# A decoder trunk on one core: the output banks of the feed-forward rotate in a fixed way, and one of the four weight sums of each quad is made by an adding DMA that GpSimd issues

## The chip, the cores and the metric

The kernel runs on one core of a Trainium2 chip. The metric is device time in microseconds (us) of one execution; the median of several runs is compared. All data are fp32.

## What is computed

A trunk of two layers on 256 tokens of width 2048. The mixers differ (retention and pooling in layer 0, windowed attention in layer 1), and the change does not touch them. What it touches is the feed-forward that follows each mixer, with 5632 hidden channels:

```python
def conv_glu_ffn(x, w_in, conv_w, conv_b, w_out):
    S = x.shape[1]
    h = x @ w_in                                    # 2048 -> 2*5632
    hp = jnp.pad(h, ((0, 0), (CONV_WIDTH - 1, 0), (0, 0)))
    hc = conv_b + hp[:, 0:S] * conv_w[0]
    for kk in range(1, CONV_WIDTH):
        hc = hc + hp[:, kk:kk + S] * conv_w[kk]
    gate, val = jnp.split(hc, 2, axis=-1)
    return (jax.nn.gelu(gate, approximate=False) * val) @ w_out
```

## The kernel before

**Precision in two parts.** TensorE multiplies in a rounded fp32 form. So each operand is split into a high part (ScalarE copies it into that form: `high`, L564, for weights) and a low part (VectorE subtracts the high part from the original: `low`, L921), and three products (high by high, low by high, high by low) make one.

**Weights** come in blocks of 1 MB (128 partitions, 4 rows of 512 columns each), numbered by a step `s`. SyncE loads them (`load`, L406) one after the other into a ring `raw` of six slots; a slot is loaded again when TensorE has used the block that was in it (semaphore `used`). ScalarE and VectorE work on blocks four and three steps ahead of TensorE (`HI_LEAD`, `LO_LEAD`). Each engine goes through its instructions in order.

**The feed-forward of a layer** is cut into 11 chunks of 512 hidden channels. A chunk c has a gate part (`G_AT[c]`, four steps) and a value part (`V_AT[c]`, four steps). In each, TensorE makes the hidden values of both in four PSUM banks (`hidden`, L1555 and L1565); ScalarE copies one half of the result out (`halves`, L628, called by `kind_halves`), VectorE adds the other (`pair_sum`, L951, called by `kind_sums`), and both do the convolution (L733 on ScalarE, L1183 on VectorE), the gelu (L706) and the product of gate and value.

**The output product** runs on two finished chunks at a time, a duo p. It takes a 2x2 scheme with seven products in place of eight: `quad(q, ...)`, one over the first half of the output columns (at `Q_AT[p]`, after the value part of chunk a = 2p+2) and one over the second (at `C_AT[p]`, after the value part of chunk b = 2p+3). There are 18 quads in all: five first and four second ones in each layer; the last duo's second half is made plainly by `pair_output`. The seven products (steps q to q+6) use W_11, W_22 and W_21 as loaded and four sums of the blocks:

```
SUM_12  = W_11 + W_12'          (arena)     first_weight_sum, L1245
SUM_24  = W_12' + W_22          (in place, in the ring slot of W_12')  weight_sums, L1251
SUM_124 = SUM_12 + W_22         (arena)     weight_sums, L1254
SUM_ALL = SUM_124 + W_21        (arena)     last_weight_sum, L1261
```

where W_12' is the block loaded at step `q + SUM_24`. All four are made by VectorE; the steps of the sums that go into the products wait on the semaphore `summed` in `high`. The activations' combinations ("forms": L1217 to L1233, L746, L1211) are made in the gate part of chunk a. Each product is read from PSUM and added to the residual `xres` by `take_product` (L1271), nine reads in a quad, counted by `quad_read`. VectorE makes the first three sums within `gate_and_sums`, while TensorE is in the value part before the quad; the three `low` of steps q, q+1 and q+2 stand behind them.

**Banks.** Eight banks, used as two sets of four, 0 to 3 and 4 to 7. Before the change a first quad of duo p has its products in set x = 4 (p % 2), and the gate part of chunk b, which follows it, goes into the same set x; so TensorE waits there until VectorE has read the quad (`quad_read`, r+7 and r+9), or, in the last duo, so does `pair_output`. The value part of chunk a stands in the other set y, and VectorE adds it (`kind_sums(a, 1, y)`) after the quad.

Of the kernel before, what the change touches and what calls it, by code (L numbers as in the profile page):

```python
# [22 lines left out]
ALU = mybir.AluOpType  # L23
# [80 lines left out]

SUM_12, W_11, SUM_24, W_22, SUM_124, W_21, SUM_ALL = range(PRODUCTS)
SUM_PLACES = {SUM_12: 1, SUM_124: 0, SUM_ALL: 1}
SUM_COUNTS = {SUM_12: 1, SUM_24: 2, SUM_124: 3, SUM_ALL: 4}
QUADS = [(l, p, n) for l in range(2) for p in range(DUOS) for n in ((0, 1) if p < DUOS - 1 else (0,))]
QUAD_AT = [S_FFN[l] + (Q_AT[p] if n == 0 else C_AT[p]) for l, p, n in QUADS]
SUMS = {s + i: (i, 4 * k + n) for k, s in enumerate(QUAD_AT) for i, n in SUM_COUNTS.items()}  # L110
SLOT_OF = [s for s in range(S_END) if s not in SUMS or SUMS[s][0] == SUM_24]
LOAD_OF = {s: i for i, s in enumerate(SLOT_OF)}

# [50 lines left out]
def build_trunk(nc, x, ln_gain, ln_bias, even_w_in, pool_w, pool_scale, even_w_out, attn_w_qkv, attn_b_qkv,  # L164
# [10 lines left out]
    with ExitStack() as ctx:  # L175
# [137 lines left out]
        g_ready = sem("g_ready")  # L313
        ffn_added = sem("ffn_added")
        summed = sem("summed")
        formed = sem("formed")
        form_hi = sem("form_hi")
        form_ready = sem("form_ready")
# [214 lines left out]
        @block.gpsimd  # L533
        def _(pool):
            nc.gpsimd.memset(ident[:], 0.0).then_inc(ident_ready, 1)
            pool.wait_ge(ident_ready, 1)
            nc.gpsimd.affine_select(out=ident[:], in_=ident[:], compare_op=ALU.not_equal, fill=1.0, base=0,
                                    pattern=[[-1, P]], channel_multiplier=1).then_inc(ident_ready, 1)


            pool.wait_ge(gain_ready, 4)
            for i, n in enumerate((2, 3)):
                c = slice(COLS * n, COLS * n + COLS)
                pool.wait_ge(last_normed, i + 1)
                pool.wait_ge(last_first, 1)
                nc.gpsimd.tensor_tensor(xres[:, 0, c], xres[:, 0, c], lnp[:, 0, c], ALU.mult).then_inc(pool_step, 1)
                pool.wait_ge(pool_step, i + 1)
                nc.gpsimd.tensor_tensor(xres[:, 0, c], xres[:, 0, c], lnp[:, 1, c], ALU.add).then_inc(last_scaled, 1)
# [3 lines left out]
        def _(act):  # L552
            def high(s):

                if s >= S_END:
                    return
                if s in SUMS:
                    act.wait_ge(summed, SUMS[s][1])
                else:
                    act.wait_ge(*landed(s))  # L560
                if s >= RING:

                    act.wait_ge(used, s - RING + 1)
                nc.scalar.activation(w_hi[:, s % RING], raw_at(s), ACT.Copy).then_inc(hi_ready, 1)  # L564
# [144 lines left out]
            def feed_forward(l):  # L709
# [76 lines left out]
                            form_high(0, f)  # L786

                for p in range(DUOS):
                    a, b, x = 2 * p + 2, 2 * p + 3, 4 * (p % 2)
                    y = 4 - x  # L790
                    s = base + G_AT[a]
                    if p == 0:
                        kind_halves(1, 1, 4, s)
                    first_taps(a - 1, 1)
                    for j in range(KG):
                        high(s + j + HI_LEAD)
                        if p > 0 and j == 0:
                            act.wait_ge(used, s)
                            for f in forms_of(p)[:-5]:
                                form_high(p, f)  # L800
                        if j == 2:
                            form_high(p, X_12)
                            form_high(p, X_22)
                        if j == 3:
                            for f in (D_1, D_2, D_4):
                                form_high(p, f)
                    s = base + V_AT[a]
                    kind_halves(a, 0, x, s)
                    first_taps(a, 0)
                    for j in range(KG):  # L810
                        high(s + j + HI_LEAD)
                        if j in (1, 2):
                            chunk_gelu(a, j - 1)
                    kind_halves(a, 1, y, base + V_AT[a] + KG)
                    s = base + Q_AT[p]
                    for j in range(PRODUCTS):
                        high(s + j + HI_LEAD)
                    first_taps(a, 1)
                    if b < FC:
                        s = base + G_AT[b]  # L820
                        for j in range(KG):
                            high(s + j + HI_LEAD)
                        s = base + V_AT[b]
                        kind_halves(b, 0, x, s)
                        first_taps(b, 0)
                        for j in range(KG):
                            high(s + j + HI_LEAD)
                            if j in (1, 2):
                                chunk_gelu(b, j - 1)
                        s = base + C_AT[p]  # L830
                        kind_halves(b, 1, y, s)
                        for j in range(PRODUCTS):
                            high(s + j + HI_LEAD)

# [71 lines left out]
        def _(dve):  # L906
# [257 lines left out]
            def feed_forward(l):  # L1164
# [83 lines left out]
                def weight_sums(q):  # L1248

                    dve.wait_ge(*landed(q + W_22))  # L1250
                    vec.tensor_tensor(raw_at(q + SUM_24), raw_at(q + SUM_24), raw_at(q + W_22), ALU.add) \  # L1251
                        .then_inc(summed, 1)
                    dve.wait_ge(summed, 4 * QUAD_AT.index(q) + 1)
                    vec.tensor_tensor(raw_at(q + SUM_124), raw_at(q + SUM_12), raw_at(q + W_22), ALU.add) \  # L1254
                        .then_inc(summed, 1)

                def last_weight_sum(q):

                    dve.wait_ge(*landed(q + W_21))
                    dve.wait_ge(summed, 4 * QUAD_AT.index(q) + 3)  # L1260
                    vec.tensor_tensor(raw_at(q + SUM_ALL), raw_at(q + SUM_124), raw_at(q + W_21), ALU.add) \  # L1261
                        .then_inc(summed, 1)

# [67 lines left out]
                        first_forms(0)  # L1331

                for p in range(DUOS):
                    a, b, x = 2 * p + 2, 2 * p + 3, 4 * (p % 2)
                    y = 4 - x
                    s = base + G_AT[a]
                    if p == 0:
                        kind_sums(1, 1, 4)
# [3 lines left out]
                    for j in range(KG):  # L1342
# [4 lines left out]
                            second_forms(p)  # L1347
                        if j == 3:
                            last_forms(p)
                    gate_and_sums(base + V_AT[a], a, x, base + Q_AT[p])  # L1350
                    quad(base + Q_AT[p], x)
                    if b < FC:
                        s = base + G_AT[b]
                        kind_sums(a, 1, y)
                        for j in range(KG):
                            low(s + j + LO_LEAD)
                            if j < 2:
                                value_pair(a, j)
                        gate_and_sums(base + V_AT[b], b, x, base + C_AT[p])
                        kind_sums(b, 1, y)  # L1360
                        quad(base + C_AT[p], x)

                tail, c = base + TAIL_AT, FC - 1
                s = base + C_AT[DUOS - 1]
                kind_sums(c, 1, 4)
                for j in range(KG):
                    if j < 2:
                        value_pair(c, j)
                    low(s + j + LO_LEAD)
                    if j == 1:  # L1370
                        gated_low(0)
                    if j == 2:
                        gated_low(1)
                        dve.wait_ge(used, s + 2)
                        add_chunk(2, 0, ffn_added)
                dve.wait_ge(used, tail)
                add_chunk(3, 2, ffn_added)
                low(tail + LO_LEAD)

                m, out0, s1 = 2 * l + 1, outs + 2, tail + NCH  # L1380
# [152 lines left out]
        def _(pe):  # L1533
# [355 lines left out]
            def feed_forward(l):  # L1889
# [60 lines left out]
                hidden(G_AT[1], 0, evicted(0, 0))  # L1950
                hidden(V_AT[1], 4, evicted(0, 1))
                for p in range(DUOS):
                    a, b, x = 2 * p + 2, 2 * p + 3, 4 * (p % 2)
                    y, q = 4 - x, base + Q_AT[p]
                    r = READS * QUAD_AT.index(q)
                    hidden(G_AT[a], x, evicted(a - 1, 0 if p == 0 else 1))
                    hidden(V_AT[a], y, evicted(1, 1) if p == 0 else ((quad_read, r - 2), (quad_read, r)))
                    quad(q, x, p, evicted(a, 0))
                    waits = ((quad_read, r + 7), (quad_read, r + READS))
                    if b < FC:  # L1960
                        hidden(G_AT[b], x, waits)
                        hidden(V_AT[b], y, evicted(a, 1))
                        quad(base + C_AT[p], x, p, evicted(b, 0))
                    else:
                        pair_output(p, x, waits)

                s, c = base + TAIL_AT, FC - 1
                pe.wait_ge(g_ready, 2 * l + 2)
                pe.wait_ge(*evicted(c, 1)[1])
                ready(s)  # L1970
                for a in range(TOK):
                    ins = plain_tile(s, T, 0, last_bank(0) + a, a, True, True)
# [148 lines left out]
```

## Time and profile before

| | us |
|---|---|
| median of 3 runs | 2020.44 (2020.44 to 2020.65) |
| the profiled execution | 2020.72 |
| its span | 2018.9 |
| busy: TensorE (PE) / VectorE (DVE) / ScalarE (ACT) / GpSimd (POOL) | 2005.5 / 1689.0 / 1081.6 / 5.8 |
| idle of TensorE in the span | 13.4 |

How to read it: "PE" is the matmuls, "PEld" the weight loads of TensorE, which overlap them; "SPq" is SyncE's DMA queue. The time of an execution is that of its span and 1.8 us around it. The rows further down give starts in us from the span's start, durations in us, and in brackets how long an engine sat idle before the row and what ended that. A matmul's row is longer than the distance to the next one's start, since matmuls are pipelined; the pace of TensorE is read from the starts.

### The profile page before, as it was taken

The page shows a single profiled execution, that of the slowest core. Times are in us where ns is not written, and L with a number is a line of the kernel's source. Part 1 is how long each engine was busy: PE and PEld are TensorE (multiplying, and loading weights), DVE is VectorE, ACT ScalarE, POOL GpSimd, SP SyncE. Part 2 cuts the span into 40 slices and gives each one's busy share as a digit, 9 for nine tenths or more (in the row PEclk, how much of TensorE's full clock was granted, in tenths as well). Part 3 has the DMA queues.
Part 4 walks back from the last instruction along what each step waited for, and adds up shares of the span by engine and source line. Part 5 has one row for each costly group of instructions (what it writes and reads, how often), then busy time and mean ns, then how long its engine had stood idle before and what let it go on. Part 6 is the DMA issues. An engine that isn't in the chain of part 4 may idle for free.

```text
span 2018.9 us, 25760 instructions
## 1 busy us (share of the span) xinstructions
PE 2005.5 (99%) x10708; PEld 1715.5 (85%) x10708; DVE 1689.0 (84%) x1705; ACT 1081.6 (54%) x1087; POOL 5.8 (0%) x10
## 2 busy tenths in 40 slices
PE   9999999999999999999999999999999999999998
PEld 8888888888888888888888877888888888888886
DVE  5446566769899998999997786776989999899998
ACT  5443444555655656556544664455565565655653
POOL 0000000000000000000000000000000000000001
PEclk9999999999999999999999999999999999999999
DMA  9654464656656556556656345465665655655662
GB/s 330 194 189 153 158 236 160 208 188 200 214 172 207 196 200 203 193 189 208 225 194 197 127 133 188 158 208 188 203 213 171 205 199 197 205 191 190 207 226 107
DMA packets 194824, 390.39 MB, mean 193 GB/s; under 512 B 6970, under 2 KB 9748, under 8 KB 193684
## 3 DMA queue, kind: packets, MB, share of 16 engines
q1 hardware_dynamic: 194419, 388.49, 57.8%
q8 instruction: 84, 1.38, 0.3%
q10 hardware_dynamic: 288, 0.26, 0.1%
q14 instruction: 33, 0.26, 0.0%
HBM read 386.36 MB, written 2.10 MB: 192 GB/s over the span
## 4 chain that ended last, share of the span: by engine, by line
PE 66%; DVE 27%; issue 5%; DMA 1%; ACT 0%; SPq 0%; DVEq 0%
PE ps L1555 26%; PE ps L1565 13%; DVE w_lo L921 9%; PE ps L1582 6%; PE ps L1584 5%; PE ps L1583 5%; DVE sum_lo L921 4%; DVE xres L1271 3%; DVE arena L1183 2%; PE ps L1884 2%; PE ps L1885 2%; PE ps L1886 2%; DVE forms L1211 1%; DVE arena L951 1%; DVE arena L1254 1%
## 5 line engine op out<-in xcount | busy, mean ns | idle before, releaser
L921 DVE TENSOR_TENSOR w_lo<-raw,w_hi 128x2048 fp32r<-128x2048 f32 x352 | 797.0, 2284 | 61.2 <-ACT w_hi L564 60.9
L564 ACT ACTIVATE w_hi<-raw 128x2048 fp32r<-128x2048 f32 x352 | 664.4, 1910 | 261.5 <-DMA raw<-ffn_w_in 100.5
L1555 PE MATMUL ps<-T,w_hi 128*128 128x512 f32 x3264 | 765.4, 390 | 2.9 <-DVE xres L1271 2.9
L1555 PEld LDWEIGHTS ps<-T,w_hi 128*128 128x128 f32 x3264 | 605.2, 188 | 128.0 <-issue 7.0
L1565 PEld LDWEIGHTS ps<-T,w_lo 128*128 128x128 f32 x3264 | 405.8, 191 | 10.0 <-issue 2.0
L1565 PE MATMUL ps<-T,w_lo 128*128 128x256 f32 x3264 | 410.6, 283 | 0.0
L1884 PE MATMUL ps<-w_hi,forms 128*128 128x512 f32 x464 | 180.5, 389 | 0.0
L1886 PE MATMUL ps<-w_hi,forms 128*128 128x512 f32 x464 | 180.5, 389 | 0.0
L1582 PE MATMUL ps<-w_hi,T 128*128 128x512 f32 (+1 forms) x448 | 177.3, 396 | 0.2
L1584 PE MATMUL ps<-w_hi,T 128*128 128x512 f32 (+1 forms) x448 | 173.8, 388 | 0.0
L1583 PE MATMUL ps<-w_lo,T 128*128 128x512 f32 (+1 forms) x448 | 173.6, 387 | 0.0
L564 ACT ACTIVATE w_hi<-arena 128x2048 fp32r<-128x2048 f32 x54 | 103.8, 1923 | 122.2 <-DVE arena L1245 83.2
L1183 DVE SCALAR_TENSOR_TENSOR arena<-arena,taps 128x256 f32<-128x256 f32 x352 | 154.6, 481 | 8.2 <-ACT arena L733 5.1
L733 ACT ACTIVATE arena<-arena,taps 128x256 f32<-128x256 f32 x176 | 91.6, 593 | 122.2 <-DVE arena L951 122.2
L951 DVE TENSOR_TENSOR arena<-ps,half 128x512 f32<-128x512 f32 x96 | 61.8, 685 | 100.2 <-ACT half L628 100.2
L628 ACT ACTIVATE half<-ps 128x512 f32<-128x512 f32 x104 | 56.3, 593 | 152.8 <-PE ps L1555 152.8
L921 DVE TENSOR_TENSOR sum_lo<-arena,w_hi 128x2048 fp32r<-128x2048 f32 x54 | 123.4, 2285 | 0.0
L1271 DVE SCALAR_TENSOR_TENSOR xres<-ps,xres 128x512 f32<-128x512 f32 x162 | 104.9, 684 | 3.0 <-PE ps L1886 3.0
L1884 PEld LDWEIGHTS ps<-w_hi,forms 128*128 128x128 f32 x464 | 87.1, 188 | 18.0
L1886 PEld LDWEIGHTS ps<-w_hi,forms 128*128 128x128 f32 x464 | 87.1, 188 | 18.0
L1582 PEld LDWEIGHTS ps<-w_hi,T 128*128 128x128 f32 x448 | 84.2, 188 | 19.8 <-DVE T L1012 2.8
L1584 PEld LDWEIGHTS ps<-w_hi,T 128*128 128x128 f32 x448 | 84.1, 188 | 17.6
(185 smaller groups left out, 1640.1 us busy)
## 6 DMA issues: line engine op xcount, KB each, us to landing
raw<-ffn_w_in SPq DMA_DIRECT2D x176, 1024.0 KB, 5.1
raw<-ffn_w_out SPq DMA_DIRECT2D x88, 1024.0 KB, 5.1
raw<-even_w_in SPq DMA_DIRECT2D x38, 1024.0 KB, 5.1
raw<-attn_w_qkv SPq DMA_DIRECT2D x20, 1024.0 KB, 5.1
raw<-even_w_out SPq DMA_DIRECT2D x16, 1024.0 KB, 5.1
raw<-attn_w_out SPq DMA_DIRECT2D x16, 1024.0 KB, 5.1
arena<-ln_gain SPq DMA_DIRECT2D x4, 1024.0 KB, 4.9
arena<-ln_bias SPq DMA_DIRECT2D x4, 1024.0 KB, 7.2
```

Of the source, the lines that this page charges most:

```text
L564: nc.scalar.activation(w_hi[:, s % RING], raw_at(s), ACT.Copy).then_inc(hi_ready, 1)
L733: ins = nc.scalar.activation(to[:, t], h[:, t, 0:SEQ], ACT.Identity, bias=taps[:, 4 * l + 3, at:at + 1], scale=taps[:, 4 * l, at:at + 1])
L921: vec.tensor_tensor(lo_at(s), raw_at(s), w_hi[:, s % RING].bitcast(F32), ALU.subtract).then_inc(lo_ready, 1)
L1183: ins = vec.scalar_tensor_tensor(conv[:, i], h[:, i, k:k + SEQ], tap(k), conv[:, i], ALU.mult, ALU.add)
L1271: vec.scalar_tensor_tensor(xres[:, a, c], ps[:, bank], sign / ALPHA, xres[:, a, c], ALU.mult, ALU.add).then_inc(quad_read, 1)
L1555: ins = mm(ps[:, banks[j]], w_hi[:, s % RING, k, P * j:P * j + P], T[:, GK * kg + k], start=kg == 0 and k == 0, stop=kg == KG - 1 and k == ...
L1565: ins = mm(ps[:, banks[j], 0:SEQ], lo_at(s)[:, k, P * j:P * j + P], T[:, GK * kg + k, 0:SEQ], start=False, stop=False)
L1582: mm(ps[:, bank, 0:n], x_hi, w_hi[:, s % RING, k, c], start=start and k == 0, stop=False)
L1583: mm(ps[:, bank, 0:n], x_hi, lo_at(s)[:, k, c], start=False, stop=False)
L1584: ins = mm(ps[:, bank, 0:n], x_lo, w_hi[:, s % RING, k, c], start=False, stop=stop and k == GK - 1)
L1884: mm(ps[:, bank], x_hi, w, start=start and k == 0, stop=False, skip_group_check=more)
L1886: ins = mm(ps[:, bank], x_lo, w, start=False, stop=last, skip_group_check=more)
```

## The change

Two things, in every feed-forward:

1. **Banks.** The sets no longer alternate with p. The gate part of a is in 0 to 3, its value part in 4 to 7, the first quad in 0 to 3, the gate part of b in 4 to 7, its value part in 0 to 3, the second quad in 4 to 7. The gate part of b now waits until the value part of a has been evicted, the value part of b waits for the reads of the first quad. `kind_sums(a, 1, 4)` and `kind_sums(b, 1, 0)` stand ahead of the quad in VectorE's order. `pair_output` and what follows it move to 4 to 7 too.
2. **SUM_24.** VectorE's addition (L1251) goes. In its place GpSimd issues two DMAs that read W_22 from HBM once more and add it to the ring slot that holds W_12' (each two of the four rows, 512 KB). The first waits until W_12' has landed and until SUM_12 has been made (which reads the same slot); the second waits until the first has landed. ScalarE's `high` of the step q+2 waits for both (`second_summed`).

```diff
-SUM_COUNTS = {SUM_12: 1, SUM_24: 2, SUM_124: 3, SUM_ALL: 4}
+SUM_COUNTS = {SUM_12: 1, SUM_24: 0, SUM_124: 2, SUM_ALL: 3}
...
 (GpSimd)
+            for k, (l, p, n) in enumerate(QUADS):
+                to = raw_at(QUAD_AT[k] + SUM_24)
+                pool.wait_ge(*landed(QUAD_AT[k] + SUM_24))
+                pool.wait_ge(summed, 3 * k + 1)
+                for j in range(2):
+                    t, c = GK * (2 * p + 1) + 2 * j, COLS * (2 * n + 1)
+                    pool.dma_start(to[:, 2 * j:2 * j + 2], w_ffn_out[l][:, t:t + 2, c:c + COLS],
+                                   accum_op=ALU.add).then_inc(second_summed, 16)
+                    pool.wait_ge(second_summed, 32 * k + 16 * (j + 1))
...
 (ScalarE, high)
-                if s in SUMS:
+                if s in SUMS and SUMS[s][0] == SUM_24:
+                    act.wait_ge(second_summed, 32 * (QUAD_AT.index(s - SUM_24) + 1))
+                elif s in SUMS:
                     act.wait_ge(summed, SUMS[s][1])
...
 (VectorE, weight_sums)
                     dve.wait_ge(*landed(q + W_22))
-                    vec.tensor_tensor(raw_at(q + SUM_24), raw_at(q + SUM_24), raw_at(q + W_22), ALU.add) \
-                        .then_inc(summed, 1)
...
 (VectorE, the loop over duos)
-                    gate_and_sums(base + V_AT[a], a, x, base + Q_AT[p])
-                    quad(base + Q_AT[p], x)
+                    gate_and_sums(base + V_AT[a], a, 0, base + Q_AT[p])
+                    kind_sums(a, 1, 4)
+                    quad(base + Q_AT[p], 0)
                     if b < FC:
                         s = base + G_AT[b]
-                        kind_sums(a, 1, y)
...
-                add_chunk(3, 2, ffn_added)
+                add_chunk(3, 6, ffn_added)
...
 (TensorE, the loop over duos)
-                    hidden(G_AT[a], x, evicted(a - 1, 0 if p == 0 else 1))
-                    hidden(V_AT[a], y, evicted(1, 1) if p == 0 else ((quad_read, r - 2), (quad_read, r)))
-                    quad(q, x, p, evicted(a, 0))
+                    hidden(G_AT[a], 0, evicted(a - 1, 0 if p == 0 else 1))
+                    hidden(V_AT[a], 4, evicted(1, 1) if p == 0 else ((quad_read, r - 2), (quad_read, r)))
+                    quad(q, 0, p, evicted(a, 0))
                     waits = ((quad_read, r + 7), (quad_read, r + READS))
                     if b < FC:
-                        hidden(G_AT[b], x, waits)
-                        hidden(V_AT[b], y, evicted(a, 1))
-                        quad(base + C_AT[p], x, p, evicted(b, 0))
+                        hidden(G_AT[b], 4, evicted(a, 1))
+                        hidden(V_AT[b], 0, waits)
+                        quad(base + C_AT[p], 4, p, evicted(b, 0))
                     else:
-                        pair_output(p, x, waits)
+                        pair_output(p, 4, evicted(a, 1))
```

The rest is the same bank numbers on ScalarE's side, the counts of `summed` (three to a quad), and in the tail a wait on `ffn_added` in place of the last eviction.

## Rows read from the trace of the kernel before

**Rows 1.** The page: busy time of each engine, and TensorE's granted clock in 40 slices.
```profile
PE 2005.5 (99%) x10708; PEld 1715.5 (85%) x10708; DVE 1689.0 (84%) x1705; ACT 1081.6 (54%) x1087; POOL 5.8 (0%) x10
...
PEclk9999999999999999999999999999999999999999
```

**Rows 2.** TensorE's waits: line, releaser, total us, times, longest us.
```profile
PE ps L1555 <- DVE xres L1271: 2.9, 6, 0.5
PE ps L1884 <- DVE xres L1271: 1.8, 2, 0.9
```

**Rows 3.** Timeline, PE: around a gate part, and around pair_output.
```profile
877.62 0.39 PE L1885 MATMUL ps<-sum_lo,forms 128*128 128x512 f32 x1
877.85 0.39 PE L1886 MATMUL ps<-w_hi,forms 128*128 128x512 f32 x1
878.72 1.63 PE L1555 MATMUL ps<-T,w_hi 128*128 128x512 f32 x6 [0.49 <-DVE xres L1271]
...
1005.61 0.39 PE L1886 MATMUL ps<-w_hi,forms 128*128 128x512 f32 x1
1006.90 0.47 PE L1884 MATMUL ps<-w_hi,gT 128*128 128x512 f32 x1 [0.90 <-DVE xres L1271]
```

**Rows 4.** Timeline, DVE, ahead of and in the second quad at 923 us.
```profile
907.02 2.28 DVE L1245 TENSOR_TENSOR arena<-raw 128x2048 f32<-128x2048 f32 x1
...
912.07 2.29 DVE L1251 TENSOR_TENSOR raw<-raw 128x2048 f32<-128x2048 f32 x1 [1.06 <-DMA raw<-ffn_w_out]
...
918.68 4.49 DVE L921 TENSOR_TENSOR w_lo<-raw,w_hi 128x2048 fp32r<-128x2048 f32 x2
924.13 1.29 DVE L951 TENSOR_TENSOR arena<-ps,half 128x512 f32<-128x512 f32 x2 [0.96 <-ACT half L628]
...
930.34 2.29 DVE L921 TENSOR_TENSOR sum_lo<-arena,w_hi 128x2048 fp32r<-128x2048 f32 x1
```

**Rows 5.** Timeline, ACT, of the same stretch.
```profile
914.39 1.92 ACT L564 ACTIVATE w_hi<-raw 128x2048 fp32r<-128x2048 f32 x1 [0.82 <-DVE raw L1251]
916.22 0.61 ACT L706 ACTIVATE arena<-arena 128x512 f32<-128x512 f32 x1
...
923.50 1.09 ACT L628 ACTIVATE half<-ps 128x512 f32<-128x512 f32 x2 [4.86 <-PE ps L1555]
```

**Rows 6.** Timeline, PE: the first matmuls of this quad and of its second step.
```profile
923.30 0.39 PE L1884 MATMUL ps<-w_hi,forms 128*128 128x512 f32 x1
...
926.02 0.39 PE L1884 MATMUL ps<-w_hi,gT 128*128 128x512 f32 x1
```

**Rows 7.** Timeline, DVE, ahead of the first quad at 987 us.
```profile
969.23 1.28 DVE L951 TENSOR_TENSOR arena<-ps,half 128x512 f32<-128x512 f32 x2
...
974.34 2.29 DVE L1245 TENSOR_TENSOR arena<-raw 128x2048 f32<-128x2048 f32 x1
...
984.86 6.69 DVE L921 TENSOR_TENSOR w_lo<-raw,w_hi 128x2048 fp32r<-128x2048 f32 x3
```

**Rows 8.** Timeline, PE: the first matmul of that quad.
```profile
986.79 0.39 PE L1884 MATMUL ps<-w_hi,forms 128*128 128x512 f32 x1
```

**Rows 9.** Timelines, DVE and PE: SUM_12 and quad start at 460 and at 591 us.
```profile
460.26 2.29 DVE L1245 TENSOR_TENSOR arena<-raw 128x2048 f32<-128x2048 f32 x1
...
476.54 0.39 PE L1884 MATMUL ps<-w_hi,forms 128*128 128x512 f32 x1
...
590.66 2.29 DVE L1245 TENSOR_TENSOR arena<-raw 128x2048 f32<-128x2048 f32 x1
...
603.53 0.39 PE L1884 MATMUL ps<-w_hi,forms 128*128 128x512 f32 x1
```

**Rows 10.** The page: a DMA queue (packets, MB, share), and issues with us to landing.
```profile
q1 hardware_dynamic: 194419, 388.49, 57.8%
...
raw<-ffn_w_out SPq DMA_DIRECT2D x88, 1024.0 KB, 5.1
```

**Rows 11.** The DMA issues: a store of half a block from SBUF.
```profile
out<-xres SPq DMA_DIRECT2D x2, 512.0 KB, 2.7
```

**Rows 12.** Busy time by stretch; the last two are DMA share and GB/s.
```profile
912.00:918.00 6.00, 6.00 (x37) 5.34 (x36) 5.93 (x3) 5.18 (x5) 0.00 (x0) 1.00 0.57 175
```

More of the change, by code:

```diff
@@ L106 @@
 SUM_PLACES = {SUM_12: 1, SUM_124: 0, SUM_ALL: 1}
-SUM_COUNTS = {SUM_12: 1, SUM_24: 2, SUM_124: 3, SUM_ALL: 4}
+SUM_COUNTS = {SUM_12: 1, SUM_24: 0, SUM_124: 2, SUM_ALL: 3}
 QUADS = [(l, p, n) for l in range(2) for p in range(DUOS) for n in ((0, 1) if p < DUOS - 1 else (0,))]
 QUAD_AT = [S_FFN[l] + (Q_AT[p] if n == 0 else C_AT[p]) for l, p, n in QUADS]
-SUMS = {s + i: (i, 4 * k + n) for k, s in enumerate(QUAD_AT) for i, n in SUM_COUNTS.items()}
+SUMS = {s + i: (i, 3 * k + n) for k, s in enumerate(QUAD_AT) for i, n in SUM_COUNTS.items()}
 SLOT_OF = [s for s in range(S_END) if s not in SUMS or SUMS[s][0] == SUM_24]
@@ L315, in build_trunk @@
         summed = sem("summed")
+        second_summed = sem("second_summed")
         formed = sem("formed")
@@ L788, in feed_forward @@
                 for p in range(DUOS):
-                    a, b, x = 2 * p + 2, 2 * p + 3, 4 * (p % 2)
-                    y = 4 - x
+                    a, b = 2 * p + 2, 2 * p + 3
                     s = base + G_AT[a]
@@ L807, in feed_forward @@
                     s = base + V_AT[a]
-                    kind_halves(a, 0, x, s)
+                    kind_halves(a, 0, 0, s)
                     first_taps(a, 0)
@@ L813, in feed_forward @@
                             chunk_gelu(a, j - 1)
-                    kind_halves(a, 1, y, base + V_AT[a] + KG)
+                    kind_halves(a, 1, 4, base + V_AT[a] + KG)
                     s = base + Q_AT[p]
@@ L823, in feed_forward @@
                         s = base + V_AT[b]
-                        kind_halves(b, 0, x, s)
+                        kind_halves(b, 0, 4, s)
                         first_taps(b, 0)
@@ L830, in feed_forward @@
                         s = base + C_AT[p]
-                        kind_halves(b, 1, y, s)
+                        kind_halves(b, 1, 0, s)
                         for j in range(PRODUCTS):
@@ L1250, in weight_sums @@
                     dve.wait_ge(*landed(q + W_22))
-                    vec.tensor_tensor(raw_at(q + SUM_24), raw_at(q + SUM_24), raw_at(q + W_22), ALU.add) \
-                        .then_inc(summed, 1)
-                    dve.wait_ge(summed, 4 * QUAD_AT.index(q) + 1)
+                    dve.wait_ge(summed, 3 * QUAD_AT.index(q) + 1)
                     vec.tensor_tensor(raw_at(q + SUM_124), raw_at(q + SUM_12), raw_at(q + W_22), ALU.add) \
@@ L1259, in last_weight_sum @@
                     dve.wait_ge(*landed(q + W_21))
-                    dve.wait_ge(summed, 4 * QUAD_AT.index(q) + 3)
+                    dve.wait_ge(summed, 3 * QUAD_AT.index(q) + 2)
                     vec.tensor_tensor(raw_at(q + SUM_ALL), raw_at(q + SUM_124), raw_at(q + W_21), ALU.add) \
@@ L1333, in feed_forward @@
                 for p in range(DUOS):
-                    a, b, x = 2 * p + 2, 2 * p + 3, 4 * (p % 2)
-                    y = 4 - x
+                    a, b = 2 * p + 2, 2 * p + 3
                     s = base + G_AT[a]
@@ L1358, in feed_forward @@
                                 value_pair(a, j)
-                        gate_and_sums(base + V_AT[b], b, x, base + C_AT[p])
-                        kind_sums(b, 1, y)
-                        quad(base + C_AT[p], x)
+                        gate_and_sums(base + V_AT[b], b, 4, base + C_AT[p])
+                        kind_sums(b, 1, 0)
+                        quad(base + C_AT[p], 4)
                 tail, c = base + TAIL_AT, FC - 1
                 s = base + C_AT[DUOS - 1]
-                kind_sums(c, 1, 4)
                 for j in range(KG):
@@ L1374, in feed_forward @@
                         dve.wait_ge(used, s + 2)
-                        add_chunk(2, 0, ffn_added)
+                        add_chunk(2, 4, ffn_added)
                 dve.wait_ge(used, tail)
-                add_chunk(3, 2, ffn_added)
+                add_chunk(3, 6, ffn_added)
                 low(tail + LO_LEAD)
@@ L1952, in feed_forward @@
                 for p in range(DUOS):
-                    a, b, x = 2 * p + 2, 2 * p + 3, 4 * (p % 2)
-                    y, q = 4 - x, base + Q_AT[p]
+                    a, b, q = 2 * p + 2, 2 * p + 3, base + Q_AT[p]
                     r = READS * QUAD_AT.index(q)
-                    hidden(G_AT[a], x, evicted(a - 1, 0 if p == 0 else 1))
-                    hidden(V_AT[a], y, evicted(1, 1) if p == 0 else ((quad_read, r - 2), (quad_read, r)))
-                    quad(q, x, p, evicted(a, 0))
+                    hidden(G_AT[a], 0, evicted(a - 1, 0 if p == 0 else 1))
+                    hidden(V_AT[a], 4, evicted(1, 1) if p == 0 else ((quad_read, r - 2), (quad_read, r)))
+                    quad(q, 0, p, evicted(a, 0))
                     waits = ((quad_read, r + 7), (quad_read, r + READS))
                     if b < FC:
-                        hidden(G_AT[b], x, waits)
-                        hidden(V_AT[b], y, evicted(a, 1))
-                        quad(base + C_AT[p], x, p, evicted(b, 0))
+                        hidden(G_AT[b], 4, evicted(a, 1))
+                        hidden(V_AT[b], 0, waits)
+                        quad(base + C_AT[p], 4, p, evicted(b, 0))
                     else:
-                        pair_output(p, x, waits)
+                        pair_output(p, 4, evicted(a, 1))
                 s, c = base + TAIL_AT, FC - 1
                 pe.wait_ge(g_ready, 2 * l + 2)
-                pe.wait_ge(*evicted(c, 1)[1])
+                pe.wait_ge(ffn_added, outs + 1)
                 ready(s)
```

## The prediction, made before the changed kernel was run

> **What bounds the kernel now.** I read the page first: TensorE is busy for 2005.5 of 2018.9 us at the full granted clock [rows 1]. So an edit on another engine can win only what TensorE still waits, 13.4 us. TensorE's waits come next: of those 13.4 us the change can reach the waits for VectorE's reads of a quad, six at 0.5 us and two at 0.9 [rows 2]. The timelines show the price of each. From the last matmul of a quad to the first of the gate part it is 0.87 us where the pace is 0.23, so 0.64 us lost; ahead of `pair_output` it is 1.29, so 1.06 lost [rows 3]. VectorE is busy for 1689.0 us [rows 1], but in no other place of the feed-forward does TensorE wait for it. That it is nearly full there matters for what follows, not for the time now.
>
> **Part 1, the banks.** The gate part of b goes into the set that held the value part of a. That has been read by `kind_sums(a, 1, 4)` early in the quad, so the wait is met. The value part of b goes into the quad's set four steps (22 us) later, long after the reads. It removes 6 x 0.64 + 2 x 1.06 = 6.0 us. What is late next: in the first quad `kind_sums(a, 1, 4)` now stands before the low part of step q+3. The second quads already work so: their sums at 924.13 wait for ScalarE's halves, and the low part of step q+4 then ends at 932.63 [rows 4]. TensorE starts a quad at 923.30 and needs 2.72 us a step [rows 6], so it wants this at 934.2: 1.6 us of margin. First quads get the same order and I cost the move at nothing; if the margin were gone, each microsecond beyond would cost one in ten quads.
>
> **Part 2, VectorE's share.** 18 additions of 2.29 us leave VectorE [rows 4], 41 us in all. They buy nothing by themselves: the waits that VectorE causes are those of part 1, and ahead of a second quad the saved time turns into a longer idle before 924.13, where it waits for the halves in any case [rows 4]. I cost this at 0.
>
> **Part 2, the adding DMAs.** The sum now comes T after SUM_12 is ready, with T the time of two DMAs in series. ScalarE's high part of step q+2 waits for it, and behind that wait stand, in order, a gelu, the high part of q+3, and the halves of the value part; VectorE's sums wait for these halves, and all low parts of the quad stand behind the sums. How large may T be? After the DMA: high 1.9, gelu 0.6, high 1.9 (like the first), then the halves, so the halves start 4.4 us after it [rows 5]. From the start of the halves (923.50) to the end of the low part of q+4 it is 9.13 us [rows 4, 5], and that is wanted at 934.2. So the DMAs may end at 934.2 - 9.13 - 4.4 = 920.7, that is 2.6 us before the quad starts, at no cost. SUM_12 ends at 909.30, so T may be 11.4 us here [rows 4, 6]. It is the same in ten quads (first of them 462.55 against 476.54 [rows 9]): all second quads and the first quad of each layer. In the eight others VectorE comes late out of the forms: its sums of the gate part are at 969.23, and SUM_12 ends at 976.63, with the quad at 986.79 [rows 7, 8]. T may be 7.6 us there, and 8.0 in six of the eight (592.95 against 603.53 [rows 9]). Beyond the allowance each microsecond is one microsecond of TensorE in each quad, since the order cannot give way. One relief: where the second quad before it has stalled, TensorE has used up the 1.6 us of margin, so VectorE enters the next stretch less late, and the eight may take some 9.5.
>
> **What is T?** The trace has no DMA of GpSimd and none that adds, so I bound it. One queue moved 388.49 MB in 57.8% of 16 engines' time [rows 10]: 0.578 x 2018.9 / 388.49 = 3.0 us per MB, 3.15 us for a block of 1.05 MB, and with 5.1 us to landing [rows 10] about 1.95 is fixed. Below: an add that costs no more than a copy of 512 KB is 1.95 + 1.6 = 3.5 us (a store of this size took 2.7 [rows 11]); two make 7.0, or 5.4 by the store. Middle: each adding half reads 512 KB of W_22 and 512 KB of the slot, as many bytes as a whole block, 5.1 us; two make 10.2. Above: SyncE's loads hold 57% of the DMA engines in this stretch [rows 12], and if the add gets only the remaining 43%, it is 1.95 + 3.15 / 0.43 = 9.3, two 18.6. In 12 us only two loads fall, which take 6.3 us of the engines, and partly in the pauses of the add; I take a third of that on top of 10.2, T = 12.
>
> The Trainium skill, "DMA: Bandwidth & Descriptors", in the section on the anatomy of a DMA of GpSimd, fits 2.0 us and bytes by 436 GB/s: 3.2 us for 512 KB, and my estimate from it for twice the bytes is 4.4. By it T would be 6.4 to 8.8, and the sum would be 2014 to about 2022. This is a copy's price without other traffic; no row here shows it.
>
> **The sum** for T = 12: ten quads at 12 - 11.4 = 0.6 us make 6.0; eight at 12 - 9.3 = 2.7 make 21.6 (I take 9.3 for the mean of 9.2 and 9.6). 2018.9 + 27.6 - 6.0 = 2040.5 of span; the profiled execution has 1.8 around its span, and the median is 0.3 below that execution: 2042.0.
>
> **Rivals.**
> *The DMAs are short* (T up to 7.6). Nothing stalls, part 1 stays: 2020.4 - 6.0 = 2014.4. For it: the store of 2.7 us. Against: an add must read what it adds to, and two come in series. It is the rival on the other side, and it is decided at the point T = 7.6. Chance 0.24.
> *The two cancel* (T from 7.6 to 9.5): the eight quads lose 0 to 1.7 us each, 0 to 14, against the 6.0 won: 2014 to 2028, most of it near 2018. Chance 0.12.
> *GpSimd writes its descriptors slowly, or between VectorE's instructions*, and T is 16: ten quads at 4.6 and eight at 6.7 make 99.6, less 6.0: 2114. For it: VectorE is without pause there, 5.93 of 6 us [rows 12]. The Trainium skill, "SBUF — State Buffer", "Who interferes with whom", says that descriptors of GpSimd's DMAs wait while VectorE runs an instruction in a mode of two ports, but not beside an addition of two tensors. The 2.29 us for 2048 elements, one element per 1.1 ns, look like no such mode. Chance 0.14.
> *The change of banks does not win*, since the wait only moves to the low parts of the gate part of b: against it, the margins above; it would make every time 6 us longer. I count it within the others.
> The forecast, T from 9.5 to 15, 2028 to some 2095, has 0.50.
>
> **How the numbers follow.** Faster by over 0.2% (under 2016.4) is the first rival and a little of the second: 0.27. Within 0.2%, about what a measurement of this kernel can tell from no change: 0.08. Slower: 0.65. The likeliest case's own range is 2028 to 2095. The range over all reaches down to the first rival, 2013, and up to T of some 15.5, 2105; beyond that lies most of the last rival.
>
> **What would show it.** No wait of L1555 or L1884 for L1271 any more (part 1). GpSimd's DMAs: 36 issues, and their time to landing, 6 us each by the forecast. ScalarE's idle time before L564, ended by GpSimd's DMA; VectorE's before L921 or L951; and new waits of TensorE for L921 at step q+2 or q+4 of the quads, some 0.6 us in ten and 2.7 us in eight. With VectorE 41 us less busy. The forecast is wrong if the DMAs land in 3.5 us each, or if TensorE stalls elsewhere.

## The result, and the profile after

The changed kernel takes 2118.7 us (median of 4 runs, 2118.32 to 2126.02) against 2020.55 us before: 1.0494 times, interval 1.0482 to 1.0507. It is 98 us slower. I had forecast 2042 us, with a range up to 2105. The direction and the place of the new waits were right, the size was not. The profiled execution has a span of 2116.8 us, 97.9 more than before.

The page: busy times and TensorE's waits (line, releaser, total us, times, longest us), which answer to [rows 1, 2].
```profile
PE 2036.4 (96%) x10708; PEld 1728.3 (82%) x10708; DVE 1651.8 (78%) x1687; ACT 1081.3 (51%) x1087; POOL 49.7 (2%) x46
...
PE ps L1892 <- DVE xres L1281: 46.6, 31, 2.0
PE ps L1892 <- DVE w_lo L933: 25.3, 9, 4.3
```
The waits ahead of the gate part and of `pair_output` are gone: none is left on L1563, which was L1555. In their place stand 72 us of waits in the quads (L1892, which was L1884). VectorE is 37 us less busy, and TensorE's idle time grew from 13.4 to 80.4 us. That is 67 us; the other 31 are matmuls that take longer (PE busy 2036.4 for as many instructions as before).

GpSimd's timeline, at one of the ten quads with the larger allowance (SUM_12 ready at 462.3, quad from 476.3) and at one of the eight late ones (SUM_12 ready at 599.6, quad from 609.5).
```profile
462.94 1.33 POOL L548 DMA_DIRECT2D raw<-ffn_w_out  x1 [461.47 <-DVE arena L1257]
469.51 1.24 POOL L548 DMA_DIRECT2D raw<-ffn_w_out  x1 [5.24 <-DMA raw<-ffn_w_out]
...
600.29 1.20 POOL L548 DMA_DIRECT2D raw<-ffn_w_out  x1 [63.05 <-DVE arena L1257]
608.32 1.21 POOL L548 DMA_DIRECT2D raw<-ffn_w_out  x1 [6.83 <-DMA raw<-ffn_w_out]
```
The first half takes 6.6 us here and 8.0 there until the second is issued; over all it is 6.3 to 6.8 in the ten quads and 6.7 to 8.7 in the eight. ScalarE's and VectorE's timelines of the first place, and TensorE's:
```profile
475.84 1.92 ACT L577 ACTIVATE w_hi<-raw 128x2048 fp32r<-128x2048 f32 x1 [9.26 <-DMA raw<-ffn_w_out]
477.66 0.61 ACT L719 ACTIVATE arena<-arena 128x512 f32<-128x512 f32 x1
478.18 1.91 ACT L577 ACTIVATE w_hi<-raw 128x2048 fp32r<-128x2048 f32 x1
479.99 1.06 ACT L641 ACTIVATE half<-ps 128x512 f32<-128x512 f32 x2
```
```profile
477.79 2.29 DVE L933 TENSOR_TENSOR w_lo<-raw,w_hi 128x2048 fp32r<-128x2048 f32 x1 [5.98 <-ACT w_hi L577]
480.59 1.29 DVE L963 TENSOR_TENSOR arena<-ps,half 128x512 f32<-128x512 f32 x2 [0.51 <-ACT half L641]
...
486.80 2.28 DVE L933 TENSOR_TENSOR sum_lo<-arena,w_hi 128x2048 fp32r<-128x2048 f32 x1
489.00 0.68 DVE L1281 SCALAR_TENSOR_TENSOR xres<-ps,xres 128x512 f32<-128x512 f32 x1
```
```profile
487.44 0.39 PE L1894 MATMUL ps<-w_hi,forms 128*128 128x512 f32 x1
489.82 0.47 PE L1892 MATMUL ps<-w_hi,forms 128*128 128x512 f32 x1 [2.00 <-DVE xres L1281]
```
ScalarE waits until 475.84; then high, gelu, high, the halves, the sums, as the prediction's chain had it. But the end of the chain is not the low part of step q+4 (489.1). It is the read of the second product behind it (489.68): step q+4 adds to a bank that still holds this product.

The granted clock of TensorE after such a wait (busy us of PE, PEld, DVE, ACT, POOL, then the clock, DMA share, GB/s), and the pace in the second of these stretches:
```profile
831.00:833.00 2.00, 1.06 (x5) 0.92 (x6) 2.00 (x3) 2.00 (x2) 0.00 (x0) 1.00 0.86 264
833.00:836.00 3.00, 3.00 (x9) 2.32 (x8) 3.00 (x3) 3.00 (x2) 0.00 (x0) 0.51 0.44 171
```
```profile
833.69 0.63 PE L1892 MATMUL ps<-w_hi,forms 128*128 128x512 f32 x1
834.12 0.63 PE L1893 MATMUL ps<-sum_lo,forms 128*128 128x512 f32 x1
```
From 833 to 836 the clock is at half (1.2 GHz in place of 2.4) and a matmul takes 0.43 us in place of 0.23. TensorE had idled 2.0 us just before 831.9. Step q+4 takes 4.3 us here. In eight of the 18 quads it takes 4.0 to 4.4 us, in the others 2.8. Before the change the mean clock of the run was 0.999, now it is 0.989.

### The profile page after: what moved, and what is told of

It reads as the page before. It is cut to its first block, busy times and chain, and to the rows that moved or that the text cites. A ratio compares the mean times of both kernels' runs of the same rounds, so it can differ in the third digit from the quotient of the medians.

```text
span 2116.8 us, 25815 instructions
## 1 busy us (share of the span) xinstructions
PE 2036.4 (96%) x10708; PEld 1728.3 (82%) x10708; DVE 1651.8 (78%) x1687; ACT 1081.3 (51%) x1087; POOL 49.7 (2%) x46
## 4 chain that ended last, share of the span: by engine, by line
PE 56%; DVE 22%; DMA 11%; issue 8%; ACT 3%; ACTq 0%; POOLq 0%; DVEq 0%; POOL 0%
PE ps L1563 18%; DMA raw<-ffn_w_out 11%; PE ps L1573 9%; DVE w_lo L933 8%; PE ps L1590 5%; PE ps L1592 5%; PE ps L1591 5%; PE ps L1892 3%; DVE sum_lo L933 3%; PE ps L1893 2%; PE ps L1894 2%; DVE arena L1195 2%; DVE xres L1281 2%; DVE arena L963 2%; DVE arena L1257 2%
## 5 line engine op out<-in xcount | busy, mean ns | idle before, releaser
L1563 PE MATMUL ps<-T,w_hi 128*128 128x512 f32 x3264 | 764.6, 390 | 0.0
L1563 PEld LDWEIGHTS ps<-T,w_hi 128*128 128x128 f32 x3264 | 605.7, 188 | 122.9 <-issue 1.7
L1892 PE MATMUL ps<-w_hi,forms 128*128 128x512 f32 x464 | 193.4, 417 | 72.0 <-DVE xres L1281 46.6
L1894 PE MATMUL ps<-w_hi,forms 128*128 128x512 f32 x464 | 188.9, 407 | 0.0
L1892 PEld LDWEIGHTS ps<-w_hi,forms 128*128 128x128 f32 x464 | 92.1, 198 | 107.8 <-DVE w_lo L933 45.9
L1894 PEld LDWEIGHTS ps<-w_hi,forms 128*128 128x128 f32 x464 | 92.3, 199 | 20.8
L1893 PE MATMUL ps<-w_lo,forms 128*128 128x512 f32 x248 | 100.4, 405 | 0.0
L1590 PEld LDWEIGHTS ps<-w_hi,T 128*128 128x128 f32 x448 | 84.2, 188 | 19.8 <-DVE T L1024 2.8
```

The lines of the kernel that those rows point to most:

```text
L1563: ins = mm(ps[:, banks[j]], w_hi[:, s % RING, k, P * j:P * j + P], T[:, GK * kg + k], start=kg == 0 and k == 0, stop=kg == KG - 1 and k == ...
L1590: mm(ps[:, bank, 0:n], x_hi, w_hi[:, s % RING, k, c], start=start and k == 0, stop=False)
L1892: mm(ps[:, bank], x_hi, w, start=start and k == 0, stop=False, skip_group_check=more)
L1893: mm(ps[:, bank], x_hi, lo_at(s)[:, k], start=False, stop=False, skip_group_check=more)
L1894: ins = mm(ps[:, bank], x_lo, w, start=False, stop=last, skip_group_check=more)
```

## The experiments

The kernel before, run beside each, took 2020.54 to 2020.65 us. The T's are ScalarE's start of step q+2 less the end of SUM_12.

**The banks alone.** VectorE makes SUM_24 again.
```diff
+                    vec.tensor_tensor(raw_at(q + SUM_24), raw_at(q + SUM_24), raw_at(q + W_22), ALU.add) \
+                        .then_inc(summed, 1)
 (GpSimd)
-            for k, (l, p, n) in enumerate(QUADS):
...
```


> Only the fixed rotation of banks (and the order of the sums that goes with it); VectorE still makes SUM_24. Theory S (the whole loss is ScalarE's wait for the adding DMAs, and the banks win the eight waits): 2020.5 - 6.6 = 2014, no wait of L1555 or L1884's successors for the reads of a quad. Rival B (the new order of VectorE, sums of the value part ahead of the first quad, costs by itself): 2020 or above, with new waits of TensorE inside the first quads.


2018.62 us, 0.9991 (0.9982 to 1.0): only 2 us won. TensorE's waits:
```profile
PE ps L1882 <- DVE xres L1271: 2.7, 8, 0.7
```
The eight waits at the gate part are gone, and eight stand in the late first quads, at step q+4: each costs 0.40 us of pace in six of them and 0.81 in two. So the rival was right in part: the sums of the value part, 1.2 us, now stand ahead of the read that q+4 waits for, and VectorE is late there. The mended order, further down, tests this.

**The same, with SUM_24 left out.** Nobody adds; the product takes W_12' instead.
```diff
-                    vec.tensor_tensor(raw_at(q + SUM_24), raw_at(q + SUM_24), raw_at(q + W_22), ALU.add) \
-                        .then_inc(summed, 1)
```


> The banks, and SUM_24 is not made by anybody: the product takes W_12' in its place. VectorE has 41 us less to do and nothing waits in its stead. Theory S (VectorE's freed time is worth nothing, since TensorE never waits for it here once the banks rotate): the same as the banks alone, 2014. Rival V (VectorE is co-critical, the chain of waits runs 27% through it): below 2014, down to 2000.


2013.91 us, 0.9966 (0.9954 to 0.9979): the full 6.6 us, and no wait for VectorE is left. VectorE's freed time is worth 4.7 us once the banks rotate. I had put it at 0.

**The adding DMAs alone**, with the banks and the order of before.
```diff
-                    hidden(G_AT[b], 4, evicted(a, 1))
-                    hidden(V_AT[b], 0, waits)
+                    hidden(G_AT[b], x, waits)
+                    hidden(V_AT[b], y, evicted(a, 1))
...
```


> Only the adding DMAs, with the alternating banks and VectorE's old order. Theory S: the DMAs land as late as in the changed kernel, 13 to 16.5 us after SUM_12. In the ten first quads the low part of step q+3 no longer stands behind the halves and sums of the value part (some 2.1 us of chain), so 10 x 2.1 = 21 less stall, the 6.6 us of the banks come back: 2119 - 21 + 7 = 2105. Rival B (the new order is to blame): well under that, 2050 or less.


2109.22 us, 1.0441 (1.0425 to 1.0457). The whole loss is the DMAs'. With them, the new banks even cost 9.5 us. The two traces show where: with the old banks and order 14 us less are lost at steps q+1 to q+3 and 7 less at step q+4, where the clock falls in four quads and not in eight, but TensorE's waits ahead of the gate parts and `pair_output` cost 11 us more. No run changes the order alone beside the DMAs.

**Both halves issued together.**
```diff
-                    pool.wait_ge(second_summed, 32 * k + 16 * (j + 1))
+                pool.wait_ge(second_summed, 32 * (k + 1))
```


> The changed kernel, but GpSimd issues both halves at once and waits for both after. Theory L (what makes the sum late is the latency of two DMAs in series, about 6.5 us each): the second half lands some 3 to 4 us earlier, so the stall falls by 3 to 4 us in each of 18 quads, by more where TensorE's clock does not drop: 2119 - 70 = 2050 (2035 to 2065). Rival W (the bytes: the DMA engines add at a low rate beside the loads): no earlier, 2110 to 2120.


2120.48 us, 1.0494 (1.048 to 1.0509): no gain. But the test did not do what it was for, so it decides nothing between the two theories. GpSimd's timeline:
```profile
462.86 1.33 POOL L548 DMA_DIRECT2D raw<-ffn_w_out  x1 [461.39 <-DVE arena L1257]
469.43 1.24 POOL L548 DMA_DIRECT2D raw<-ffn_w_out  x1 [5.24 <-issue]
```
The second issue is as late as before, although the program has no wait there ("issue").

**The same with twice the room for descriptors** (2048 bytes).
```diff
-    nc = bacc.Bacc(..., dynamic_dma_scratch_size=1024)
+    nc = bacc.Bacc(..., dynamic_dma_scratch_size=2048)
```


> Both halves issued without a wait between them, as before, but with 2048 bytes for GpSimd's descriptors. In the run with 1024 bytes the second issue came 6.5 us after the first although nothing waited for it in the program. Theory R (it waited for room): the second issue now comes 1.3 us after the first, T is 10 to 11.5, time 2035 to 2065. Rival W (the DMA engines add at their rate, room or not): the second issue is early, but T stays over 12.5: 2095 to 2120.


2086.01 us, 1.0325 (1.0305 to 1.0345).
```profile
463.00 2.58 POOL L548 DMA_DIRECT2D raw<-ffn_w_out  x2 [461.53 <-DVE arena L1257]
526.82 1.20 POOL L548 DMA_DIRECT2D raw<-ffn_w_out  x1 [61.23 <-DVE arena L1257]
533.49 1.22 POOL L548 DMA_DIRECT2D raw<-ffn_w_out  x1 [5.48 <-issue]
```
In ten of the 18 quads the second half now follows at once and T is 10.9 to 12.7; in the others it still comes 6.3 to 8.3 us later and T is 13.4 to 14.9. So where it follows at once, room for descriptors was what it had waited for; there theory R holds, and its 2035 to 2065 was missed because of the other eight. That these still lack room in 2048 bytes is my reading; no run gave them more.

**One DMA for the whole block**, with 2048 bytes.
```diff
-                for j in range(2):
-                    pool.dma_start(to[:, 2 * j:2 * j + 2], w_ffn_out[l][:, t:t + 2, c:c + COLS],
...
+                pool.dma_start(to, w_ffn_out[l][:, t:t + GK, c:c + COLS],
...
```


> The changed kernel with one adding DMA of 1 MB in place of two halves in series, and twice the room for GpSimd's descriptors (2048 bytes). Theory L (latency, 1.2 us of issue and 2 us fixed, is paid once less): T 10 to 11, hardly a stall in ten quads, 3 to 4 us in eight: 2040 (2025 to 2060). Rival W (the adding goes by bytes): T 12.5 or more, 2095 to 2120.


2051.4 us, 1.0159 (1.0142 to 1.0176). T is 9.4 to 11.8, so the rival is out. One such DMA lands in 9.4 us where two halves took 6.3 each: a part of some 3 us is paid once less. The 4 us less of T are worth 67 us of time.

**Copying in place of adding.**
```diff
-                    pool.dma_start(to[:, 2 * j:2 * j + 2], w_ffn_out[l][:, t:t + 2, c:c + COLS],
-                                   accum_op=ALU.add).then_inc(second_summed, 16)
+                    pool.dma_start(to[:, 2 * j:2 * j + 2], w_ffn_out[l][:, t:t + 2, c:c + COLS]).then_inc(second_summed, 16)
```


> The changed kernel, but GpSimd's two DMAs copy W_22 over the slot in place of adding it. Theory A (the adding is the dear part: each packet reads twice and writes): a half lands 4 to 5 us after its issue in place of 6.3 to 8, T is 9.5 to 10.5, no stall in ten quads and about 2.5 us in eight: 2014 + 20 = 2034 (2025 to 2050). Rival G (GpSimd's way of issuing is dear, whatever the DMA does): T stays 13 to 16, 2110 to 2120.


2062.66 us, 1.021 (1.0194 to 1.0225), T 10.3 to 12.0. The queue of GpSimd's DMAs (packets, MB, share of 16 engines) and its issues, first of the changed kernel, then of this one:
```profile
q0 software_dynamic: 9792, 18.88, 5.9%
...
raw<-ffn_w_out POOLq DMA_DIRECT2D x36, 512.0 KB, 6.3
```
```profile
q0 software_dynamic: 5184, 18.88, 2.6%
...
raw<-ffn_w_out POOLq DMA_DIRECT2D x36, 512.0 KB, 5.0
```
Adding takes nearly twice the packets and 2.3 times the engines' time (5.9% of 2116.8 against 2.6% of 2061.6). It is 1.3 of the 6.3 us of a half; T falls by 3.4 us on average and 56 of the 98 us come back. The other 42 are there for a plain copy too. The theory had the landing right (5.0), but T and the time came out above its ranges: two landings and the 0.6 us before the first make 10.6 already.

**GpSimd adds with its own engine**, no DMA.
```diff
+                for j in range(GK):
+                    nc.gpsimd.tensor_tensor(to[:, j], to[:, j], other[:, j], ALU.add).then_inc(second_summed, 1)
```


> The banks, and GpSimd makes SUM_24 with four additions of its own, 128x512 each, from the two ring slots; no DMA adds. It takes 1.29 us for one at the end of the kernel before, so 5.2 us after SUM_12 or the landing of W_22: T about 5.5 to 8, inside the allowance: with VectorE freed, 2014, as without the sum. Rival P (GpSimd's reads and VectorE's two-input instructions get in each other's way): VectorE's additions of 2.29 us grow by one or more in each quad where GpSimd works, and the eight late quads stall 1 to 4 us: 2020 to 2045.


2078.25 us, 1.0286 (1.0271 to 1.0302). GpSimd's and VectorE's timelines:
```profile
465.01 11.18 POOL L549 TENSOR_TENSOR raw<-raw 128x512 f32<-128x512 f32 x4 [463.55 <-DMA raw<-ffn_w_out]
...
601.65 5.69 POOL L549 TENSOR_TENSOR raw<-raw 128x512 f32<-128x512 f32 x4 [57.16 <-DVE arena L1256]
```
```profile
464.90 2.29 DVE L1263 TENSOR_TENSOR arena<-arena,raw 128x2048 f32<-128x2048 f32 x1 [0.78 <-DMA raw<-ffn_w_out]
467.12 3.38 DVE L932 TENSOR_TENSOR sum_lo<-arena,w_hi 128x2048 fp32r<-128x2048 f32 x1
470.42 3.38 DVE L932 TENSOR_TENSOR w_lo<-raw,w_hi 128x2048 fp32r<-128x2048 f32 x1
...
601.39 4.79 DVE L1194 SCALAR_TENSOR_TENSOR arena<-arena,taps 128x256 f32<-128x256 f32 x4
```
The rival, and more of it, with a time above its range. In eleven quads GpSimd works beside VectorE's large additions and subtractions: three of its four additions take 3.3 us, the one that has no such neighbour 1.3. The four take 11.2 us in place of 5.2, T is 12.8 to 14.2, and two or three of VectorE's take 3.38 us in place of 2.28. In the other seven quads, all late ones, it works beside VectorE's convolution and takes 5.7 us for the four, and T is 5.9; but four pieces of the convolution take 4.79 us there in place of 1.80, and TensorE still waits 1.4 to 1.8 us at step q+4.

**Half by DMA, half by VectorE.**
```diff
+                t, c = GK * (2 * p + 1) + 2, COLS * (2 * n + 1)
+                pool.dma_start(to[:, 2:], w_ffn_out[l][:, t:t + 2, c:c + COLS],
+                               accum_op=ALU.add).then_inc(second_summed, 16)
...
+                    vec.tensor_tensor(raw_at(q + SUM_24)[:, :2], raw_at(q + SUM_24)[:, :2], raw_at(q + W_22)[:, :2],
+                                      ALU.add).then_inc(summed, 1)
```


> The banks, and SUM_24 shared: rows 0 and 1 of the block by VectorE (1.15 us), rows 2 and 3 by one adding DMA of 512 KB. Theory D (only the lateness of the DMA counts, beyond 3.2 us before the quad starts): it ends 6.8 us after SUM_12 in ten quads, no stall, and up to 8.5 us in the eight late ones, about 1 us beyond; 2014 + 8 = 2022. Rival E (DMAs of GpSimd cost something else as well, contention with the loads): above 2030. If it lands in 6.8 us everywhere: 2014.


2020.96 us, 1.0003 (0.9994 to 1.0012). T is 6.6 to 7.3 in ten quads, with no stall, and 7.4 to 8.8 in the eight late ones, which stall 0.3 to 1.4 us. For one of these, at step q+4:
```profile
614.11 0.39 PE L1896 MATMUL ps<-w_hi,forms 128*128 128x512 f32 x1
615.31 0.47 PE L1894 MATMUL ps<-w_hi,forms 128*128 128x512 f32 x1 [0.82 <-DVE xres L1283]
```
Here ScalarE got the sum at 601.32 and the quad started at 603.45, 2.1 us later; the stall is 1.20 - 0.23 = 0.97 us. All eight lie on one line: the stall is 3.1 us less the time from the DMA's end to the quad's start. The prediction had 2.6 for this 3.1; the read of the second product, 0.6 us, was missing.

**A quarter by DMA**, three rows by VectorE.
```diff
-                t, c = GK * (2 * p + 1) + 2, COLS * (2 * n + 1)
-                pool.dma_start(to[:, 2:], w_ffn_out[l][:, t:t + 2, c:c + COLS],
+                t, c = GK * (2 * p + 1) + 3, COLS * (2 * n + 1)
+                pool.dma_start(to[:, 3:], w_ffn_out[l][:, t:t + 1, c:c + COLS],
...
```


> As before, with three rows by VectorE (1.7 us) and one row, 256 KB, by the adding DMA. Theory D: it ends some 5.5 to 6.5 us after SUM_12, within the allowance everywhere, and VectorE saves 0.57 us where the banks alone lose 0.4 us in six quads and 0.8 in two: 2014.5. Rival E: as the banks alone or slower, 2018.6 and above.


2014.68 us, 0.9972 (0.9961 to 0.9982). T is 4.7 to 6.7, and no wait of TensorE in a quad is over 0.3 us. An adding DMA that is in time costs next to nothing: the kernel without the sum is 0.8 us faster.

**The order mended, without any DMA.**
```diff
-                    kind_sums(a, 1, 4)
-                    quad(base + Q_AT[p], 0)
+                    quad(base + Q_AT[p], 0, lambda: kind_sums(a, 1, 4))
...
                     take_product(s, x + 1, 0, 0, 1.0)
+                    between()
```


> No DMA adds. The banks alone, but the sums of the value part stand behind the second read of the first quad in VectorE's order, not ahead of the quad. Theory O (the banks alone win 2 in place of 6.6 us because these sums, 1.2 us, stand ahead of the read that step q+4 waits for): the waits of 0.4 and 0.8 us at q+4 go, at most 0.2 us comes back behind it: 2014 to 2015.5. Rival C (VectorE is late there whatever the order): 2018.6, as the banks alone.


2015.21 us, 0.9974 (0.9964 to 0.9984). The waits at q+4 are gone; 1.3 us are left of the difference to the kernel without the sum.

**The waits at q+4 filled**, in the changed kernel.
```diff
+                    for _ in range(8):
+                        mm(ps[:, x + 2], form_at(D_4)[:, 0, 0], T[:, 0], start=True, stop=True)
                     ready(s + SUM_124)
```


> The changed kernel, with eight matmuls of 512 columns more, whose result nobody reads, ahead of the wait at step q+4 of each quad, where TensorE sits idle for 2.0 us. Theory K (TensorE's clock falls to half after such idle stretches, which costs 23 of the 98 us): the idle is filled, the clock stays up in most quads, 2119 - 18 = 2101 (2095 to 2108). Rival N (the slow matmuls come from the DMA's traffic or the late data, not from the idle): 2119, or more by the matmuls that do not fit into the wait, 0 to 5 us.


2100.04 us, 1.0396 (1.0382 to 1.041): 18.7 us less with 144 matmuls more. Spans and mean granted clock of the changed kernel and of this one:
```profile
core 0: 2116.8 us, clock 0.989
```
```profile
core 0: 2098.7 us, clock 0.999
```
The clock stays up when TensorE has something to do, and step q+4 takes 2.8 us in all 18 quads. The DMAs' traffic is the same, so it was not that. Two reservations. In the three other executions of this kernel the mean clock was 0.993 to 0.994, against 0.986 to 0.988 in those of the changed kernel, so it stays up in most places, not in all. And by the two traces step q+4 and what is left of it behind give back 12.8 us; the other 5 are less time lost at q+1 to q+3, most of it in the late quads, where T is 13.6 on average in place of 14.9.

## Why the prediction was wrong

The chain from the DMA to TensorE was right: ScalarE's wait, then the gelu, the high part, the halves, the sums and the low parts, and one microsecond of TensorE for each one of lateness. With the measured 3.1 us of the second point below, the time lost at steps q+1 to q+3 is T less the allowance, to within 0.1 us in each of the 18 quads. Wrong were sizes.

- **T, the term that failed first.** I took 12 us; it was 13.1 to 16.5, on average 14.0 in the ten quads and 14.9 in the eight. The two landings of 5.1 each became 6.6 and 6.3 by the rows above, and some 8 for the first in the late quads. In the sum of "two DMAs in series" the start was missing: GpSimd issues 0.6 us after SUM_12, so T was 0.6 + 6.6 + 6.3 = 13.5 at the first place. It is busy 1.2 us with each issue, 0.7 for a copy; that is within the 6.6 and 6.3. The engines' time per byte, twice a copy's, was nearly right (2.3). That the first half is dearer in the late quads I read as the load that SyncE had issued shortly before; no run took that load away. The difference to 12 makes 10 x 2.0 + 8 x 2.9 = 43 us.
- **The allowance.** 3.1 us before the quad, not 2.6 (half by DMA, half by VectorE): 18 x 0.5 = 9 us. I had ended the chain at the low part of q+4 and overlooked the read behind it.
- **The relief** of 1.3 us in the late quads did not come: SUM_12 ends 9.9 to 11.4 us before them, 10.5 on average, as before the change (10.2 to 10.6). 8 x 1.3 = 10 us. The trace shows two kinds. Four of them follow a quad whose step q+4 ran at full clock, and SUM_12 comes 0.7 us later to the quad than before, not earlier (in the run with filled waits it is so in all eight). The other four follow one whose step q+4 ran partly at half clock, and it comes 0.8 us earlier; but there the first half takes 8.5 to 8.7 us, so the earlier start won nothing. Why the 0.7 us are lost, no run shows. And the range's lower end, 2028 at T = 9.5, was worked out without this relief, while the sum had it in.
- **The clock** was no term at all. The three points above make 62 us, the forecast's 27.6 and 6.6 for the banks bring the sum to 2018.9 + 27.6 + 62 - 6.6 = 2102; the measured span is 2116.8. Of the 15 that are left the trace shows 12.8 in the eight quads whose step q+4 takes 4.0 to 4.4 us in place of 2.8; the other 2 are 0.1 us in each quad, in which TensorE picks up its pace after a wait.
- **The banks.** The eight waits that they were to remove are gone, and in the kernel without the sum they won 6.6 us for the forecast 6.0, but only because VectorE had been relieved. In the changed kernel itself they did not win: beside the DMAs, the old banks are 9.5 us faster. "I cost the move at nothing" was wrong: alone, they win 2.0. And "VectorE's share, 0" was wrong by the same 4.7 us. The margin of 1.6 that I had read from a second quad held neither the read nor the late first quads.
- **The rivals.** "T is 16" named nearly the time (2114), but by another cause, so that was luck: an issue of GpSimd takes 1.20 us at 600.29, where VectorE is in the middle of its work, and 1.21 at 608.32, where VectorE idles, so its descriptors are not held up by VectorE. T was 14.4 on average, and the allowance and the clock made up the rest. The fit of the Trainium skill, "DMA: Bandwidth & Descriptors", in the section on the anatomy of a DMA of GpSimd, gives 3.2 us for 512 KB; the copy took 5.0 from its issue beside the loads, so here the measurement decides.

The best of the versions that compute the whole are the quarter by DMA and the mended order, 0.9972 and 0.9974, not to be told apart.

## What to carry to other kernels

When work moves off a full engine onto a DMA, its duration matters less than who waits for it in order: write down the whole chain up to the last read that frees a bank, and compare its end with the transfer's. Two DMAs in series behind a computed value cost 13 to 16 us here where the engine took 2.3. And a stall that recurs can be dearer than its length, because TensorE can come out of it at half clock: here 13 us on top of 90.

## What had not been expected of the hardware

- After idling 0.6 and then 2.0 us within one quad, TensorE ran some 3 us at a granted clock of 0.51 (the rows above). It is not so in every quad, and the idle time before does not tell which: below, after waits of 0.9 and 2.0 us the clock stayed at 1.00, and after none and 2.0 it fell. What decides, no run shows. The single waits of 0.5 to 0.9 us before the change had left it at 1.00 [rows 1 to 3].
```profile
551.80 0.47 PE L1892 MATMUL ps<-w_hi,forms 128*128 128x512 f32 x1 [0.92 <-DVE xres L1281]
...
556.81 0.47 PE L1892 MATMUL ps<-w_hi,forms 128*128 128x512 f32 x1 [2.00 <-DVE xres L1281]
...
1493.02 0.47 PE L1892 MATMUL ps<-w_hi,forms 128*128 128x512 f32 x1
...
1498.02 0.47 PE L1892 MATMUL ps<-w_hi,forms 128*128 128x512 f32 x1 [2.02 <-DVE xres L1281]
```
```profile
557.00:560.00 3.00, 3.00 (x14) 2.44 (x14) 3.00 (x3) 3.00 (x3) 0.00 (x0) 1.00 0.77 294
1499.00:1502.00 3.00, 3.00 (x9) 2.33 (x8) 3.00 (x3) 3.00 (x2) 0.00 (x0) 0.50 0.50 194
```
- With 1024 bytes for descriptors, GpSimd's second DMA comes 5.1 to 8.4 us after the end of the first one's issue, with no wait in the program; with 2048 bytes it comes at once in ten of 18 quads.
- An adding DMA of 256 KB, 512 KB and 1 MB lands 4.4, 6.3 to 6.5 and 9.4 us after its issue (median of each run), beside the loads.
- While GpSimd adds two tensors in SBUF, its addition of 128x512 takes 3.3 us beside VectorE's additions in place of 1.3, and VectorE's goes from 2.28 to 3.38; beside VectorE's convolution GpSimd's takes 1.4 to 1.5, and four pieces of the convolution 4.79 in place of 1.80.
- While the two halves are added beside the loads (from 463 to 476 us), the DMA engines are 94% busy, at 223 GB/s.
```profile
463.00:476.00 13.00, 13.00 (x74) 11.42 (x73) 7.67 (x6) 3.74 (x4) 2.51 (x2) 1.00 0.94 223
```
